# Last down product on banks of its own with gated weights, its last four steps tile by tile

## What is computed

```python
h_res = h_res + g1 * mixed
h2 = rms_norm(h_res, norm2_g[l]) * (1.0 + sc2) + sh2
ff = jnp.square(jax.nn.relu(h2 @ w_mlp_in[l])) @ w_mlp_out[l]     # (1024x4096) @ (4096x1024)
h_res = h_res + g2 * ff                                           # g2: one value per output channel
```

## Time and profile before

| what | us |
|---|---|
| median of 3 runs | 1028.45 (1027.74 to 1029.88) |
| the profiled execution's own time | 1026.16 |
| its span, first to last instruction | 1024.4 |
| TensorE matmuls busy | 932.7 (91%) |
| VectorE busy | 754.1 (74%) |
| GpSimd busy | 554.2 (54%) |
| ScalarE busy | 414.2 (40%) |
| mean DMA rate over the span | 170 GB/s |

### The profile page before, as it was taken

How to read it: one execution, slowest core, us unless ns; L and a number is a source line. 1 busy time by engine, 2 the same in 40 slices (tenths; PEclk the granted TensorE clock), 3 DMA queues, 4 the chain that set the end, 5 groups by cost and what they waited for, 6 DMA issues and landing times.

```text
span 1024.4 us, 12470 instructions
## 1 busy us (share of the span) xinstructions
PE 932.7 (91%) x4373; PEld 769.8 (75%) x4373; DVE 754.1 (74%) x997; ACT 414.2 (40%) x734; POOL 554.2 (54%) x440
## 2 busy tenths in 40 slices
PE   1779999997999899999999979999988999998997
PEld 1668878886878778777777758888866888887776
DVE  5977999978654677878887867866587443789875
ACT  1445655557555544422322212333334443432340
POOL 7454545536232435987888757854444554442543
PEclk9899999999999999999999989999999999999999
DMA  9663423203222331744555323448997628875772
GB/s 339 260 210 99 120 87 105 81 1 124 83 83 84 100 125 52 248 162 155 177 172 165 123 102 134 158 157 298 342 304 267 209 86 268 296 256 177 263 255 84
DMA packets 91982, 174.48 MB, mean 170 GB/s; under 512 B 9288, under 2 KB 26256, under 8 KB 91920
## 3 DMA queue, kind: packets, MB, share of 16 engines
q1 hardware_dynamic: 90704, 173.05, 50.2%
q10 hardware_dynamic: 1216, 0.63, 0.2%
HBM read 135.90 MB, written 37.75 MB: 170 GB/s over the span
## 4 chain that ended last, share of the span: by engine, by line
PE 44%; DVE 30%; DMA 7%; issue 5%; POOL 5%; ACT 4%; SPq 4%; POOLq 0%; DVEq 0%; ACTq 0%
PE psum L1857 14%; PE psum L1859 14%; PE psum L1858 14%; DMA down_raw<-in_w_mlp_out 5%; DVE down_operands L1579 3%; PE psum L1853 2%; SPq L578 2%; DVE act_quads_a L1500 2%; DVE acc L1339 2%; DVE act_quads_a L1539 2%; DMA slots<-in_w_ada 2%; DVE act_quads_b L1542 1%; DVE act_quads_b L1538 1%; DVE xh L1126 1%; DVE acc L1050 1%
## 5 line engine op out<-in xcount | busy, mean ns | idle before, releaser
L1817 POOL TENSOR_TENSOR down_operands<-down_raw,down_operands 128x1024 fp32r<-128x1024 f32 x48 | 124.8, 2603 | 156.1 <-ACT down_operands L968 155.9
L1857 PE MATMUL psum<-down_operands 128*128 128x512 f32 x448 | 176.9, 395 | 12.1 <-DVE down_operands L1579 12.1
L1858 PE MATMUL psum<-down_operands 128*128 128x512 f32 x448 | 175.8, 392 | 0.0
L1859 PE MATMUL psum<-down_operands 128*128 128x512 f32 x448 | 175.6, 392 | 0.0
L968 ACT CAST down_operands<-down_raw 128x1024 fp32r<-128x1024 f32 x96 | 100.7, 1052 | 172.9 <-DMA down_raw<-in_w_mlp_out 51.2
L1857 PE MATMUL psum<-h2T,w_operands 128*128 128x512 f32 x272 | 108.9, 400 | 11.7 <-DVE up_temps L1513 10.3
L1579 DVE TENSOR_TENSOR down_operands<-down_raw,down_operands 128x1024 fp32r<-128x1024 f32 x48 | 88.2, 1844 | 40.6 <-ACT down_operands L968 40.5
L1806 POOL TENSOR_TENSOR w_operands<-raw,w_operands 128x512 fp32r<-128x512 f32 x56 | 81.7, 1459 | 53.7 <-ACT w_operands L929 53.7
L1857 PEld LDWEIGHTS psum<-down_operands 128*128 128x128 f32 x448 | 84.9, 189 | 34.1 <-DVE down_operands L1579 16.5
L1859 PE MATMUL psum<-h2T,w_operands 128*128 128x512 f32 x272 | 106.7, 392 | 0.0
L1858 PE MATMUL psum<-h2T,w_operands 128*128 128x512 f32 x272 | 106.6, 392 | 0.0
(11 more groups left out here) (244 smaller groups left out, 2040.3 us busy)
## 6 DMA issues: line engine op xcount, KB each, us to landing
down_raw<-in_w_mlp_out SPq DMA_DIRECT2D x160, 256.0 KB, 4.7
down_raw<-act_scratch SPq DMA_DIRECT2D x112, 256.0 KB, 3.6
raw<-in_w_ada SPq DMA_DIRECT2D x32, 512.0 KB, 4.5
raw<-in_w_mlp_in SPq DMA_DIRECT2D x32, 512.0 KB, 4.6
act_scratch<-act_quads_a SPq DMA_DIRECT2D x64, 256.0 KB, 2.2
act_scratch<-act_quads_b SPq DMA_DIRECT2D x48, 256.0 KB, 2.0
slots<-in_w_ada SPq DMA_DIRECT2D x8, 512.0 KB, 12.7
xh<-in_x SPq DMA_DIRECT2D x8, 512.0 KB, 5.9
```

What stands on the lines that cost most here:

```text
L1817: g.tensor_tensor(o[:, 1, :, :], r[:, 0:2, :], o[:, 0, :, :].bitcast(F32), ALU.subtract).then_inc(op2_lo_pool, 1)
L1857: mm(o, wh, ah, start=first, stop=False, skip_group_check=adds)
L1858: mm(o, wh, al, start=False, stop=False, skip_group_check=adds)
L1859: return mm(o, wl, ah, start=False, stop=last, skip_group_check=adds)
```

## The change

- P3 no longer adds to P5's banks: it starts them afresh (`fresh`). What P5 left there is added to `yU` in P5's gather, "E", one instruction more per tile (the new L1604). P3's first step waits for E instead of Y22s.
- P3's W2 piece is multiplied by the gate before the cast: one VectorE instruction per step (the new L1558 in `sum_step`), and ScalarE's cast now waits for it.
- The end has no gating left: `yU` is gated and gets x2 ("Eg", "Ex"), and when a tile is complete VectorE adds its bank (one instruction), and SP stores. GpSimd's three adds are gone.
- TensorE does the last four steps (108 to 111) tile by tile: tile 0 of the four steps, then tile 1, and so on (`LAST = 4`, `down_tile`).

```diff
@@ -308,7 +308,7 @@
         step_done, tile_done = sem("step_done"), sem("tile_done")
-        y_first, y_mixed, y_added = sem("y_first_kept"), sem("y_mixed"), sem("y_added")
+        y_first, y_mixed = sem("y_first_kept"), sem("y_mixed")
         xq_in = [sem("xq_in0"), sem("xq_in1")]
@@ -341,10 +341,11 @@
         STEPS = len(DOWN) * NBLK
+        LAST = 4
         Y_STEPS = ([("U2", j) for j in range(4)] + [(n, j) for j in range(4) for n in ("Y11g", "Y11")]
-                   + [("U3", j) for j in range(4)] + [(n, j) for j in range(4) for n in ("Y22s", "Y22g", "Y22")]
+                   + [("U3", j) for j in range(4)] + [(n, j) for j in range(4) for n in ("Y22s", "E", "Y22g", "Y22")]
                    + [(n, j) for j in range(4) for n in ("Y21s", "Y21g", "Y21")]
-                   + [(n, j) for j in range(4) for n in ("Eg", "E")] + [("Y12g", j) for j in range(4)] + [("Y12", 3)])
+                   + [(n, j) for j in range(4) for n in ("Eg", "Ex")] + [("Y12", j) for j in range(4)])
         Y_COUNT = {what: n + 1 for n, what in enumerate(Y_STEPS)}
@@ -403,8 +404,8 @@
         def w2_summed_by(eng, n):
-            if step_name(n) in ("P6", "P5", "P4"):
-                eng.wait_ge(w2_summed, sum(step_name(m) in ("P6", "P5", "P4") for m in range(n + 1)))
+            if step_name(n) in ("P6", "P5", "P4", "P3"):
+                eng.wait_ge(w2_summed, sum(step_name(m) in ("P6", "P5", "P4", "P3") for m in range(n + 1)))
@@ -638,10 +639,7 @@
             for j in range(4):
-                if j < 3:
-                    sp.wait_ge(y_added, j + 1)
-                else:
-                    sp.wait_ge(y_mixed, Y_COUNT["Y12", 3])
+                sp.wait_ge(y_mixed, Y_COUNT["Y12", j])
                 sp.dma_start(out_rows[j * P:(j + 1) * P, HS:D], yU[:, j, :]).then_inc(out_quad[2], 16)
@@ -1553,9 +1551,12 @@
                 name, f, r = step_name(n), n % NBLK, raw2[n % RAWS2]
-                if name not in ("P6", "P5", "P4"):
+                if name not in ("P6", "P5", "P4", "P3"):
                     return
                 raw2_landed(dve, n)
+                if name == "P3":
+                    v.tensor_tensor(r[:, 1, :], r[:, 1, :], g2b[:, HS:D], ALU.mult).then_inc(w2_summed, 1)
+                    return
                 if name == "P6":
@@ -1600,6 +1601,7 @@
                         v.tensor_tensor(t, o, yR[:, j, :], ALU.add).then_inc(y_mixed, 1)
+                        v.tensor_tensor(yU[:, j, :], o, yU[:, j, :], ALU.add).then_inc(y_mixed, 1)
                         y_done("Y22s", j)
@@ -1623,15 +1625,15 @@
             for j in range(4):
+                y_done("E", j)
                 v.tensor_tensor(yU[:, j, :], yU[:, j, :], g2b[:, HS:D], ALU.mult).then_inc(y_mixed, 1)
...
             for j in range(4):
-                dve.wait_ge(tile_done, 4 * (STEPS - 1) + j + 1)
-                v.tensor_tensor(yR[:, j, :], bank(j), g2b[:, HS:D], ALU.mult).then_inc(y_mixed, 1)
-            y_done("Y12g", 3)
-            v.tensor_tensor(yU[:, 3, :], yU[:, 3, :], yR[:, 3, :], ALU.add).then_inc(y_mixed, 1)
+                dve.wait_ge(tile_done, 4 * (STEPS - LAST) + LAST * (j + 1))
+                y_done("Ex", j)
+                v.tensor_tensor(yU[:, j, :], bank(j), yU[:, j, :], ALU.add).then_inc(y_mixed, 1)
@@ -1840,9 +1842,6 @@
                 lo_step(n)
-            for j in range(3):
-                pool.wait_ge(y_mixed, Y_COUNT["Y12g", j])
-                g.tensor_tensor(yU[:, j, :], yU[:, j, :], yR[:, j, :], ALU.add).then_inc(y_added, 1)
@@ -2212,32 +2211,34 @@
-            def down_step(n):
+            def down_tile(n, j):
...
                 first = 4 * (p % 2)
-                fresh = name in ("P1", "P6", "P5", "P4")
+                fresh = name not in ("P2", "P7")
                 op2_made(pe, n)
                 o = op2[n % OPS2]
+                if f == 0:
+                    if name == "P1":
+                        pe.wait_ge(up_mixed, mix_count(NBLK - 2, "S4"))
+                        pe.wait_ge(c11_relu, kept_count(NBLK - 2))
+                    elif name == "P6":
+                        pe.wait_ge(up_mixed, mix_count(NBLK - 1, "S4"))
+                        pe.wait_ge(c11_relu, kept_count(NBLK - 1))
+                    elif name == "P2":
+                        pe.wait_ge(y_first, j + 1)
+                    else:
+                        pe.wait_ge(y_mixed, Y_COUNT[{"P7": "U2", "P5": "Y11g", "P4": "U3", "P3": "E"}[name], j])
+                cut = slice(j * P, (j + 1) * P)
+                three(bank(first + j), o[:, 0, 0, cut], o[:, 1, 0, cut], o[:, 0, 1, :], o[:, 1, 1, :],
+                      fresh and f == 0, f == NBLK - 1, not fresh).then_inc(tile_done, 1)
+
+            for n in range(STEPS - LAST):
                 for j in range(4):
-                    if f == 0:
-                        if name == "P1":
-                            pe.wait_ge(up_mixed, mix_count(NBLK - 2, "S4"))
-                            pe.wait_ge(c11_relu, kept_count(NBLK - 2))
-                        elif name == "P6":
-                            pe.wait_ge(up_mixed, mix_count(NBLK - 1, "S4"))
-                            pe.wait_ge(c11_relu, kept_count(NBLK - 1))
-                        elif name == "P2":
-                            pe.wait_ge(y_first, j + 1)
-                        else:
-                            pe.wait_ge(y_mixed, Y_COUNT[{"P7": "U2", "P5": "Y11g", "P4": "U3", "P3": "Y22s"}[name], j])
-                    cut = slice(j * P, (j + 1) * P)
-                    ins = three(bank(first + j), o[:, 0, 0, cut], o[:, 1, 0, cut], o[:, 0, 1, :], o[:, 1, 1, :],
-                                fresh and f == 0, f == NBLK - 1, not fresh)
-                    ins.then_inc(tile_done, 1)
-
-            for n in range(STEPS):
-                down_step(n)
+                    down_tile(n, j)
+            for j in range(4):
+                for n in range(STEPS - LAST, STEPS):
+                    down_tile(n, j)
```

## The result

| | before | changed |
|---|---|---|
| median of 7 runs each, us | 1028.45 (1027.12 to 1029.88) | 1031.96 (1031.39 to 1035.14) |
| ratio | | 1.0041 (95%: 1.0025 to 1.0056) |
| the profiled execution's own time, us | 1026.16 | 1033.47 |
| its span, us | 1024.4 | 1031.7 |

Slower by 0.41%, 4.2 us by the ratio and 3.5 by the medians. The forecast was +5.5 us, 1034.0 with a range of 1028.8 to 1037.5. In a later comparison of 12 runs the ratio was 1.0047 (1.0032 to 1.0063), 4.8 us.

The account below looks back on a forecast made before the run. TensorE's waits for VectorE's work, before steps 85 and 101, and the end after the last matmul were taken as the bound. -2.6 + 2.1 + 4.3 + 1.7 + 0 = +5.5 us on the median 1028.45: 1034.0, range 1028.8 to 1037.5.

Parts of the forecast that it names:

- The end: After the last matmul: three of four tiles added and stored earlier, no GpSimd adds; gain 2.6 us.
- Four adds: In P5's gather: each tile grows by 0.5 to 0.68 us, lengthening the wait before step 85; cost 2.1 us.
- The products: Sixteen in P3: they delay P4's gather and lengthen the wait before step 101; cost 4.3 us (-0.7 to 5.1).
- the low half of step 97: On VectorE in P3, behind the product of step 99: 1.2 us, done at 972.9, 3.2 late.
- the load of step 102: On SP, after step 97's low half: issued until 973.8, landed between 976.5 and 979.3.
- The gather's length: P4's gather on VectorE: 10.5 us instead of 13.5, with one GpSimd instruction beside it.
- The clock: TensorE's clock falls at the longer wait before step 101, with no later wait covering it; cost 1.7 us (0 to 3.4).
- The clock at step 85: Already fell there, 1.7 us lost; the later 1.57 us wait covers it, and up to 1.57 more.
- The last four steps: Steps 108 to 111 tile by tile want step 111 6.1 us earlier; cost nothing, up to 1 us.
- rival 3: New order of the last four steps adds a wait for step 110 or 111, 1 to 4 us more; chance 0.17.
- Rivals 1, 2 and 4: Products hidden, 1027.3 to 1029.0 (0.14); adds also covered, 1025.6 (0.07); clock stays up, 1032.3 (within main case's 0.62).

Follow-up runs that it names:

- adds_only: Changed kernel without the sixteen gate products in P3, each finished tile gated and then added at the end; 1027.25 us, ratio 1.0004 to the kernel before.
- adds_late: gather_spread with the four adds moved out of P5's gather to ahead of the sum of step 93; 1027.08 us, ratio 0.9991 to the kernel before.
- gather_first: Changed kernel with P4's gather ahead of the product of step 102 in VectorE's order; 1030.13 us, ratio 1.0016 to the kernel before.
- adds_late_steps: adds_late with the last four steps in the old order (LAST = 1); 1025.74 us, ratio 0.9961 to the kernel before.
- step_order: Changed kernel with the last four steps in the old order (LAST = 1); 1033.51 us, ratio 1.0052 to the kernel before.
- gather_spread: Changed kernel with P4's gather cut into tiles behind the low halves of steps 101, 103, 105 and 107; 1029.76 us, ratio 1.0013 to the kernel before.

## Why the prediction was right
The sign, the mechanism and the place were right; the size was within the interval of the ratio (forecast 1.0053, measured 1.0041 and 1.0047). That the two profiles differ by 5.58 us where 5.5 were forecast is in part luck: three terms came out 0.2 to 0.3 us lower than forecast, and the products 0.9 higher. Term by term, from the two profiles:
- **The end**, forecast -2.6: measured -2.9. The forecast had 3.5 us from the end of the last matmul; it was 3.2 (3.61 from its start, 0.39 of them the matmul).
- **Four adds**, forecast 2.1 (2.0 to 2.7): the gather grew by 1.87, 0.48 a tile, a little under the lower end of 0.5. They went into the wait before step 85 and were still there at steps 91 and 93. That later waits give nothing back held in these two; over the fourteen profiles 1.8 us are left at step 93, 1.4 in adds_only. adds_late shows that a place for them was free 15 us later. In the time of whole executions they aren't settled.
- **The products**, forecast 4.3 (-0.7 to 5.1) for step 101: measured 5.22, just above the upper bound. adds_only, without them, has a wait of 0.86 us there; and by gather_first (24.77 us from step 93 to step 101, for 28.01) 3.2 of it are due to the one product of step 102 ahead of the gather. Counted from step 93, the gather came 7.6 us later than before (15.63 for 8.04), where 5.0 to 7.5 were forecast. The step of the working that was low is the low half of step 97: it was put at 1.2 us and took 3.43, held up beside GpSimd's low half of step 98, so the load of step 102 was issued 2.6 us later than in the working (11.2 us after step 93 for 8.5). The load itself was as forecast: its product ran 3.9 us after the issue, between the 2.7 and 5.5 of the working. The gather's length, forecast 10.5, was 10.5. The one instruction held up in each gather (2.70 and 2.72 us) has two SBUF inputs. The added reads of a bank didn't meet GpSimd in the changed kernel; in adds_late GpSimd worked from 954.56 beside the last two of them, and the four took 2.48 us, no longer than the four adds at the end of adds_late_steps, which had no GpSimd beside them. The Trainium skill, page SBUF — State Buffer, section Who interferes with whom, says that a VectorE instruction with two SBUF inputs contends with a GpSimd instruction that reads SBUF, and one with a single SBUF input doesn't. The trace agrees.
- **The clock**, forecast 1.7: 1.40, from step 101 to the last matmul; seven slow matmuls, where I had looked for a dozen. That it fell was right; how much it costs varies (last section).
- **The clock at step 85**: it fell at a wait of 5.75 us too; the later start of step 91 hid it, the wait before it shrank from 1.57 to 0.65. As forecast.
- **The last four steps**, forecast nothing, up to 1: no wait in the changed kernel (step_order equal to 0.4 us). But rival 3 was real where the big wait is removed. I had put its condition wrongly: not on top of the long wait, which gives VectorE the time to get ahead, but instead of it.
- Rivals 1, 2 and 4 fell: the waits before steps 101 and 85 both grew, and the clock fell at the longer wait.
- What the sum had too high against the medians (5.5 for 3.5) isn't explained by a term: counted from the gather the difference is 5.58. The part ahead of it, where all these kernels have the same code, varies by up to 5.9 us between the profiled executions.

## What to carry to other kernels
Where TensorE waits for one engine that works through a fixed list, an instruction added to that list costs the time by which it lengthens the list (0.48 us here for one of 0.68), and one that waits for a load costs the wait as well, for all that stands behind it: put the long block that nobody waits for (the gather) behind what is waited for, or cut it up, and put additions where that engine was idle. Saving work behind the last matmul is worth having, but look for the part of the change that does it alone: here an order of four steps gave 2.2 of 2.9 us and nothing else was needed. When you work a list of instructions through by hand, check each against what the other engines do at its new time: the low half that was put at 1.2 us and took 3.43 was the largest miss of this forecast.

## What was not expected of the hardware
In the fourteen profiles, after 740 us, TensorE's clock fell at each of the 20 waits of 2.71 to 6.47 us and at 5 of the 17 between 1.78 and 2.29. At a sixth of these, 1.78 us (gather_spread, step 109), it stayed up for the next three matmuls and fell in the wait of 1.24 us right behind them. At no other wait did it fall. Sometimes it fell before TensorE restarted (first matmul 0.78 to 0.80 us), sometimes during the first matmul or up to about a microsecond and a half after it (0.50 or 0.58 first, 0.63 each later). Then 5 to 13 matmuls started 0.43 us apart instead of 0.23; with the first ones, 1.5 to 3.0 us were lost each time. I had taken 1.7 from a single one. And the same code ahead of the change brought VectorE to the gather of P5 at times 5.9 us apart, more than the whole effect of the change.
